# Sixteen experts' weights in a ring of four places: the landing of the next expert reported between the loads, gate and up weights loaded behind the last gate product

## What is computed

```python
hid = jax.nn.silu(jnp.einsum('td,edf->tef', t, w_gate)) * jnp.einsum('td,edf->tef', t, w_up)
hid = hid * combine[..., None].astype(hid.dtype)
y = jnp.einsum('tef,efd->td', hid, w_down)
```

## Time and profile before

| what | us |
|---|---|
| median of 3 runs | 2327.17 |
| lowest and highest run | 2324.61, 2339.4 |
| profiled execution | 2330.84 |
| its span | 2328.9 |
| TensorE busy (16471 matmuls) | 2119.4 |
| VectorE busy | 992.8 |
| ScalarE busy | 627.9 |
| POOL busy | 251.0 |
| gate and up products, line 1160 (x560) | 255.4 |
| down products, line 1170 (x280) | 126.2 |

### The profile page before, as it was taken

One profiled execution on the slowest core, in us unless ns is written; L12 is line 12 of the kernel. 1 busy time (PEld: TensorE's weight loads), 2 busy tenths in 40 slices (PEclk: granted clock), 3 DMA queues, 4 the chain that ended last, 5 costly groups with the idle time before them and its releaser, 6 DMA issues. The chain is left out here.

```text
span 2328.9 us, 39352 instructions
## 1 busy us (share of the span) xinstructions
PE 2119.4 (91%) x16471; PEld 1295.2 (56%) x16471; DVE 992.8 (43%) x1846; ACT 627.9 (27%) x1292; POOL 251.0 (11%) x311
## 2 busy tenths in 40 slices
PE   4996899999998889998899999999999689989993
PEld 3555567766554478887654555555455544434441
DVE  3254565652776476667460111001233423323334
ACT  6222666663343233332330000000111011111113
POOL 2000000000000133342000000000000012212220
PEclk8998899999999999999999999999999589999997
DMA  9422200001100223433302211111422656787846
GB/s 332 150 94 90 58 4 2 2 1 55 27 23 5 39 48 65 74 61 51 84 0 73 51 31 27 27 27 46 155 83 98 226 151 171 194 242 207 241 85 207
DMA packets 256381, 210.09 MB, mean 90 GB/s; under 512 B 147468, under 2 KB 219472, under 8 KB 255568
## 3 DMA queue, kind: packets, MB, share of 16 engines
q1 hardware_dynamic: 244912, 168.66, 24.6%
q0 software_dynamic: 11296, 38.92, 7.4%
HBM read 160.14 MB, written 47.25 MB: 89 GB/s over the span
## 5 line engine op out<-in xcount | busy, mean ns | idle before, releaser
L800 PE MATMUL ps<-R 128*128 128x512 f32 (+1 forms) x816 | 297.4, 522 | 5.0 <-DVE R L1526 1.9
L1076 PE MATMUL ps<-R 128*128 128x512 f32 (+1 forms) x768 | 279.5, 522 | 4.4 <-POOLq L2186 2.3
L1160 PE MATMUL ps<-R 128*128 x560 | 255.4, 610 | 16.2 <-SPq L691 13.9
L800 PEld LDWEIGHTS ps<-R 128*128 128x128 f32 x816 | 154.3, 190 | 144.5 <-issue 133.7
L1076 PEld LDWEIGHTS ps<-R 128*128 128x128 f32 x768 | 145.3, 190 | 136.1 <-issue 126.3
L1160 PEld LDWEIGHTS ps<-R 128*128 128x128 f32 x560 | 109.1, 196 | 156.8 <-issue 156.8
L1850 DVE TENSOR_TENSOR R<-ps,R 128x512 f32<-128x512 f32 (+1 forms) x48 | 28.9, 603 | 376.8 <-ACT R L1426 376.0
L1589 DVE TENSOR_SCALAR_CACHE_REDUCE R<-ps 128x512 f32<-128x512 f32 (+1 forms) x208 | 128.4, 666 | 60.1 <-PE ps L896 60.0
L968 PE MATMUL ps<-R 64*64 64x64 f32 x3840 | 130.0, 225 | 24.7 <-DMA R<-tu_scratch 13.0
L968 PEld LDWEIGHTS ps<-R 64*64 64x64 f32 x3840 | 122.8, 140 | 42.5 <-issue 13.7
L1101 PE MATMUL ps<-R 128*128 128x512 f32 x320 | 141.2, 600 | 3.9 <-PEq L1088 3.9
(11 more groups left out here) (288 smaller groups left out, 2800.0 us busy)
## 6 DMA issues: line engine op xcount, KB each, us to landing
R<-in_w_mod_dram SPq DMA_DIRECT2D x12, 2048.0 KB, 9.1
R<-in_w_gate_e_dram SPq DMA_DIRECT2D x16, 1024.0 KB, 5.8
R<-in_w_up_e_dram SPq DMA_DIRECT2D x16, 1024.0 KB, 11.2
R<-in_w_down_e_dram SPq DMA_DIRECT2D x16, 1024.0 KB, 13.2
R<-in_w_in_dram SPq DMA_DIRECT2D x30, 512.0 KB, 5.4
R<-tu_scratch SPq DMA_DIRECT2D x80, 128.0 KB, 3.3
R<-in_x_sample_dram SPq DMA_DIRECT2D x16, 512.0 KB, 6.3
lt_scratch<-R SPq DMA_DIRECT2D x40, 128.0 KB, 2.8
```

Source lines behind the costliest of these rows:

```text
L800: last = mm(ps[:, u % 4, 0:w], w_sb[n % NW][:, k, :], hT[:, k, c0:c0 + w], start=(k == 0), stop=(k == KD - 1))
L1076: mm(ps[:, o + x, 0:w], wk[:, x, k, :], hT[:, k, c0:c0 + w], start=(k == 0), stop=(k == KD - 1))
L1160: last = mm(ps[:, 2 + t % 2, :], hsT[t % 2][:, k, :], R[:, bass.ds(at + (RB + k * 512), 512)], start=(k == 0), stop=(k == KD - 1))
```

## The change

Four things differ. `expert_load` is split into `gate_up_load` (two DMAs) and `down_load` (one). The wait for an expert's landing with its report becomes `expert_landed`, and the report of expert e+1 stands between the two parts of the load. The gate and up weights of a new expert are loaded when the gate products of the expert that had the place are done (`gu_mm`, counted in tiles); the down weights when its down products are done (`dn_mm`, in halves), as before. The table gets 16 more columns, since both counts are wanted, and DVE one more copy.

```diff
--- before.py
+++ after.py
@@ -445,14 +445,14 @@
         r_pos = rsc(2, NT)
         r_hi, r_lo, tok_f = rsc(2 * NT), rsc(2 * NT), rsc(2 * NT)
         r_ge, r_hot = rsc(2 * NT, MT + 1), rsc(2 * NT, MT)
-        r_tab = rsc(HT + MT + NE)
+        r_tab = rsc(HT + MT + 2 * NE)
         r_hot_w = flat(r_ge)[:, 0:2 * NT * MT].rearrange("p (j t) -> p j t", t=MT)
         r_lane = R3[:, 11520:11520 + 2 * NT * P].rearrange("p (j c) -> p j c", c=P)
         assert rat[0] <= 8192
         slot_i = sb("slot_i", [P, MT], U32)
         put_i = sb("put_i", [P, MT], U32)
         tok_i = sb("tok_i", [P, 2, NT], I32)
-        tab_i = sb("tab_i", [P, HT + MT + NE], I32)
+        tab_i = sb("tab_i", [P, HT + MT + 2 * NE], I32)
         nf_row = R3[:, 14080:14080 + 1024]
         wts = sb("wts", [P, 2, NT])
         Y_IN = (0, 1, 2, 2, 3, 3, 4, 5, 6, 7)
@@ -665,13 +665,23 @@
                 x2_store(n - 2)
                 h2_store(n - 2)
 
-            def expert_load(e):
+            def gate_up_load(e):
                 b = ew[e % RING_E]
                 for half, name in enumerate(("w_gate_e", "w_up_e")):
                     sp.dma_start(b[:, 0:4096].rearrange("p (k n) -> p k n", k=KD)[:, :, half * FF:(half + 1) * FF],
                                  a[name][0, e].rearrange("(k p) f -> p k f", p=P)).then_inc(S[f"ew_in{e % RING_E}"], 16)
-                sp.dma_start(b[:, 4096:6144].rearrange("p (k n) -> p k n", k=2),
+
+            def down_load(e):
+                sp.dma_start(ew[e % RING_E][:, 4096:6144].rearrange("p (k n) -> p k n", k=2),
                              a["w_down_e"][0, e].rearrange("(k p) n -> p k n", p=P)).then_inc(S[f"ew_in{e % RING_E}"], 16)
+
+            def expert_load(e):
+                gate_up_load(e)
+                down_load(e)
+
+            def expert_landed(e):
+                sp.wait_ge(S[f"ew_in{e % RING_E}"], landed(e, RING_E, 3))
+                sp.sem_inc(S["ew_ready"], 1)
 
             sp.wait_ge(S["out_used"], NT)
             rows_load(R1[:, 6144:8192], 6, 2)
@@ -686,13 +696,19 @@
             for n in (NT - 2, NT - 1):
                 sp.wait_ge(S[f"h2_out{n % 2}"], landed(n, 2))
             expert_load(3)
+            expert_landed(0)
             for e in range(NE):
-                sp.wait_ge(S[f"ew_in{e % RING_E}"], landed(e, RING_E, 3))
-                sp.sem_inc(S["ew_ready"], 1)
-                if 1 <= e and e + RING_E - 1 < NE:
-                    through = sp.value_load(tab_i[0:1, HT + MT + e - 1:HT + MT + e], min_val=2, max_val=2 * MT)
-                    sp.wait_ge(S["dn_mm"], through)
-                    expert_load(e + RING_E - 1)
+                new = e + RING_E - 1 if 1 <= e < NE - RING_E + 1 else None
+                if new is not None:
+                    tiles_through = sp.value_load(tab_i[0:1, HT + MT + e - 1:HT + MT + e], min_val=1, max_val=MT)
+                    sp.wait_ge(S["gu_mm"], tiles_through)
+                    gate_up_load(new)
+                if e + 1 < NE:
+                    expert_landed(e + 1)
+                if new is not None:
+                    halves_through = sp.value_load(tab_i[0:1, HT + MT + NE + e - 1:HT + MT + NE + e], min_val=2, max_val=2 * MT)
+                    sp.wait_ge(S["dn_mm"], halves_through)
+                    down_load(new)
 
             sp.sem_inc(S["arrivals"], 1)
             sp.wait_ge(S["arrivals"], 5 * 7)
@@ -2002,7 +2018,9 @@
             dve.wait_ge(S["dve_chain"], count("dve_chain"))
             v.tensor_reduce(r_tab[:, 0:HT], ends, AX.X, ALU.add).then_inc(S["dve_chain"], 1)
             dve.wait_ge(S["dve_chain"], count("dve_chain"))
-            v.tensor_scalar(r_tab[:, HT + MT:], r_nt, 2.0, None, ALU.mult).then_inc(S["dve_chain"], 1)
+            v.tensor_copy(r_tab[:, HT + MT:HT + MT + NE], r_nt).then_inc(S["dve_chain"], 1)
+            dve.wait_ge(S["dve_chain"], count("dve_chain"))
+            v.tensor_scalar(r_tab[:, HT + MT + NE:], r_nt, 2.0, None, ALU.mult).then_inc(S["dve_chain"], 1)
             dve.wait_ge(S["dve_chain"], count("dve_chain"))
             v.tensor_copy(tab_i[:], r_tab).then_inc(S["dve_chain"], 1)
             dve.wait_ge(S["dve_chain"], count("dve_chain"))
```

## The result

| what | before | after |
|---|---|---|
| median of 10 runs, us | 2332.11 | 2315.38 |
| lowest and highest run, us | 2324.61, 2339.4 | 2306.03, 2319.26 |
| span of the profiled execution, us | 2328.9 | 2313.7 |
| start of tile 0's gate products, us | 1866.22 | 1868.96 |
| tile 0 to tile 1, gate starts, us | 12.80 | 13.01 |

The ratio is 0.9925, interval 0.991 to 0.9939, which is 17.5 us less, between 14.2 and 21.0; the medians lie 16.7 us apart. Beside the ten runs of after, before's median is 2332.11, 4.9 us above the three runs that the forecast started from. A second series of five rounds on another occasion gave 0.9918 (0.9898 to 0.9937).

The account below looks back on a forecast made before the run. TensorE in the expert stage, 35 tiles x 11.39 us plus interruptions by SP's late reports; -6.37 - 13.24 + 0 + 0 = -19.6 us from the 2327.17 median gave 2307.6 us, 0.84% less, range 2301 to 2319.

Parts of the forecast that it names:

- The sum: Expert stage: 6.37 us gained at tile 4, 13.24 at tiles 15 to 17, other terms 0, together 19.6 us less.
- waits of 12.27 us on line 691: TensorE stands before the gate products of tiles 4, 15, 16 and 17 until SP reports the expert's weights: 12.27 us.
- slow groups: Gate groups after the four stops exceed 7.03 us, the clock being at 1.2 GHz after stops: 6.67 us.
- refilling: TensorE filling up again after the four stops: 0.67 us.
- Report between the loads: SP reports expert e+1 a turn earlier, removing the stops: 6.37 us at tile 4, 13.24 us at tiles 15 to 17.
- Gate and up weights early: Loads leave up to 16 us earlier, after the last gate product; alone worth nothing, only making the reports early.
- The signs: Expected profile: one SP wait of 1.6 us, gate starts 11.39 us apart, full clock, gate and up loads right behind gate groups.
- Value load, DVE, tile 0: SP's second value load, about 0.27 us 12 times, and DVE's extra copy cost nothing; tile 0's 1.63 us wait stays.
- Rival 1, the clock is not given back: Waits go but slow gate groups stay, caused by something else such as the transfer burst: 2314.2 us, chance 0.05.
- rival 4: Slower: earlier gate and up loads delay the gathers, 4.9 us a stop with 12 loads, 2367 us; chance 0.03.
- Rival 2, the DMA engines pace the burst: Transfers stretch tiles 15 to 17 to 13.0 us each, losing 4.8 us of the gain: 2312.4 us, chance 0.08.
- Rivals 3: SP sits waiting for expert e+1's landing, the down load behind it, and reports no earlier: 2327 us, chance 0.04.

Follow-up runs that it names:

- report_between: The changed kernel with gate and up loads again waiting for the down products, the report still between the loads; tile 1 to tile 34 382.15 us, ratio 0.9952.
- early_report_last: The changed kernel, early gate and up loads kept, with the next expert's report behind the down load; tile 1 to tile 34 379.65 us, ratio 0.9931.

## Why the prediction was right

**The sum.** Put: 19.6 us off tile 1 to tile 34. Measured: 19.58. The mechanism was right, issues of SP ahead of a report that could have been made earlier, and each term answers to a row: waits of 12.27 us on line 691, gone; 6.67 us of slow groups, gone with them (all 7.03 us from tile 2 on); 0.67 us of refilling, gone. The forecast of 2307.6 against 2315.4 is off by 7.8 us, of which 4.9 are the median of before, which moved from 2327.17 with three runs to 2332.11 with ten; the remaining 2.9 are inside the interval of the ratio. The range from 2301 to 2319 had been widened for such a shift and held it, with 3.6 us to spare. In relative terms, 0.84% was put, 0.75% measured.

**Report between the loads.** The margins put for tile 16, 8.4 us, and tile 17, 7.9, came out as 9.2 and 8.1. The first is larger since three issues that are spread out take 0.37, 0.37 and 0.58 us, not the 2.98 of three in a row. The second agrees in part by luck: I had let the landing of expert 8's down weights, 14.9 us after their issue, decide it. They landed 5.0 us after it, and SP's own issues set the report.

**Gate and up weights early: the step that was wrong.** I had put: "so this alone is worth nothing; it only makes the reports early." The second half holds: in the changed kernel, the reports come in time only by it, and `report_between`, without it, is 5.98 us longer. The first half does not: alone it is worth 16.10 us (`early_report_last`). I had looked for TensorE waiting for weights and found none, but the loads cost TensorE by their place on SP's queue, as the stops in front of the reports did. The total came out right all the same, because it was the sum of the stops, and all four went, whichever part took them away. What is worth nothing is the early loads on top of a report ahead of everything (376.17 beside 376.16).

**The signs.** The gate and up loads left right behind a gate group for 8 of the 12 experts; those of experts 5, 9, 10 and 11 were held by the down load ahead of them. And the stage was not without a gap between the five waits: tile 1 waits 2.25 us for ScalarE, before and after, which is the rest of the 16.2 us of the earlier trace rows.

**Value load, DVE, tile 0.** The first two show nowhere on TensorE's path (DVE still waits 4.93 us for the one-hot products ahead of `slot_i`); tile 0's wait stayed, 1.57 us.

**Rival 1, the clock is not given back.** Fell: with the DMA share at 1.06 the clock is 1.00 and no group is slow. But not every stop lowered it. Stops of 0.61, 1.24, 2.21 and 2.62 us were followed by groups of 7.13, and so was tile 1's of 2.25 us in all eleven profiled executions that have it. The nine stops of 3.08 to 3.75 us were followed by groups of 8.8 us or more, and so were two of 2.20 and 2.46 us. From 2.20 to 2.62 us, then, the length of the stop did not decide. So my even 4.9 us for a stop, used in rival 4, holds for the long ones alone.

**Rival 2, the DMA engines pace the burst.** The load on them was sized rightly: 13.0 us of transfers for each 11.39 us period is 1.14, and the windows show 1.05 to 1.06, three periods in a row. What I had not put is that SP's issues get long meanwhile, 6.77 us for one up load at 2066.02 (with the report first 6.36 and 5.81 us for two down loads). That the surplus of transfers is what holds them up is inferred from the two coming together. TensorE did not notice, for the report behind it was not wanted before tile 20. Gathers took at most 8.7 us and scatters 10.3, against 8.2 and 10.7 before: their slack was not touched, and the rule of the shared engines in the Trainium skill, DMA: Bandwidth & Descriptors, "Issuing engines are not separate DMA queues", which nothing here contradicts, had nothing on TensorE's path to act on.

**Rivals 3 and 4.** No report waited for a landing to TensorE's cost, and no gather was late.

## What to carry to other kernels

A report (a wait for a landing and an increment) on an in-order queue costs what is ahead of it on that queue: look for the wait that ends just before the consumer starts, and move the report ahead of it; here one moved line gave all of 19.6 us. The more elaborate half of the change would have given 16.1 by itself and gave nothing on top of that line, so try the parts of a change one by one and not only their sum: a load for whose data nobody waits can still cost by its place on the queue. Count a stall of TensorE with the slow group behind it, but read the clock for each, since the stops of 0.61 and 1.24 us brought no slow group. And measure such a change by the stretch that it touches: here start to start of the same instruction repeated to 0.01 us where the median of ten runs moves by several.

## What the runs showed of the hardware that I had not expected

- **A DMA issue on SP has no fixed duration.** The down weights' 1 MB took 0.37 us to issue apart, 1.94 as the third of three, and an up load 6.77 us after a period with a DMA share of 1.06. In halves, six issues took 3.2 us where three took 3.0. Behind such a 6.8 us issue the next report, expert 9's, came at 2072.8 at the earliest. It was wanted by tile 20; had expert 8 had one tile only, tile 18 would have wanted it at 2075.8, and 3 us of margin would have been left instead of 8.
- **Filling a wait can be worth more than its work.** Eight transposes put into TensorE's wait ahead of tile 0 took their own 1.04 us and a 2.25 us wait off the path between tile 0 and tile 1, for a start of tile 0 that is 1.5 us later, and the group behind them ran at full clock from its start, 2.7 us less. That the clock rose because of the transposes is inferred from one profile; in the other profiled executions without them tile 0's group took 8.85 to 9.89 us.
